# Prompt attention in a hybrid decoder step: each tile's scaling of its probabilities moved one place later in VectorE's order

## The reference

```
s = (q_lat . c + q_pe . k_pe) * MLA_SCALE
s = where(k_pos <= q_pos, s, -inf)
p = softmax(s)
out = p . c
```

## Time and profile before

| | us |
|---|---|
| timed runs | 1011.88, 1012.37, 1013.96 |
| median | 1012.37 |
| profiled execution, its time | 1013.96 |
| profiled execution, its span in the trace | 1012.2 |
| granted TensorE clock, mean over the span | 0.987 of 2.4 GHz |

### The profile page before, as it was taken

How to read it: one execution, slowest core, us unless ns; L and a number is a source line. 1 busy time by engine, 2 the same in 40 slices (tenths; PEclk the granted TensorE clock), 3 DMA queues, 4 the chain that set the end, 5 groups by cost and what they waited for, 6 DMA issues and landing times.

```text
span 1012.2 us, 20658 instructions
## 1 busy us (share of the span) xinstructions
PE 974.0 (96%) x8604; PEld 846.5 (84%) x8604; DVE 513.6 (51%) x980; ACT 444.4 (44%) x964; POOL 157.2 (16%) x257
## 2 busy tenths in 40 slices
PE   4999999999988999999999999999999999999997
PEld 3988899877756656666665999999999999999996
DVE  5655766666467387545546443533343344334333
ACT  5545638566644776544445324421332133113212
POOL 1020500155530301354550000000000000000000
PEclk9999969999999999999999999999999999999999
DMA  7312111030023602577772322332222222222202
GB/s 251 120 51 84 43 42 42 14 99 10 2 53 95 250 1 75 194 238 247 272 239 93 128 72 76 105 104 84 84 84 84 84 84 84 88 101 104 84 1 89
DMA packets 31655, 102.58 MB, mean 101 GB/s; under 512 B 14023, under 2 KB 14967, under 8 KB 25218
## 3 DMA queue, kind: packets, MB, share of 16 engines
q1 hardware_dynamic: 22346, 63.50, 19.1%
q0 software_dynamic: 9216, 37.75, 11.0%
HBM read 96.45 MB, written 4.22 MB: 99 GB/s over the span
## 4 chain that ended last, share of the span: by engine, by line
PE 90%; DVE 3%; ACT 3%; issue 1%; DMA 1%; SPq 0%; DVEq 0%; ACTq 0%
PE PS L598 17%; PE PS L600 17%; PE PS L599 17%; PE PS L1082 7%; PE PS L1093 3%; PE PS L1119 3%; PE PS L733 2%; PE PS L988 2%; PE PS L1102 1%; PE PS L806 1%; PE PS L837 1%; PE PS L889 1%; PE PS L1026 1%; PE PS L1007 1%; DMA RAW<-in_w_stream 1%
## 5 line engine op out<-in xcount | busy, mean ns | idle before, releaser
L598 PE MATMUL PS<-XH,WH 128*128 128x272 f32 (+1 forms) x896 | 261.8, 292 | 0.0
L600 PE MATMUL PS<-XH,WL 128*128 128x272 f32 (+1 forms) x896 | 261.2, 291 | 0.0
L599 PE MATMUL PS<-XL,WH 128*128 128x272 f32 (+1 forms) x896 | 260.2, 290 | 0.0
L1255 ACT ACTIVATE WH<-RAW 128x2048 fp32r<-128x2048 f32 x46 | 88.0, 1913 | 195.9 <-PE PS L600 191.7
L598 PEld LDWEIGHTS PS<-XH,WH 128*128 128x128 f32 x896 | 169.7, 189 | 4.8 <-issue 4.2
L599 PEld LDWEIGHTS PS<-XL,WH 128*128 128x128 f32 x896 | 170.0, 190 | 0.0
L600 PEld LDWEIGHTS PS<-XH,WL 128*128 128x128 f32 x896 | 169.7, 189 | 0.0
L598 PE MATMUL PS<-NH,WH 128*128 128x272 f32 x512 | 149.2, 291 | 0.8 <-DVE WL L1771 0.8
L600 PE MATMUL PS<-NH,WL 128*128 128x272 f32 x512 | 147.7, 289 | 0.0
L599 PE MATMUL PS<-NL,WH 128*128 128x272 f32 x512 | 146.7, 287 | 0.0
L1771 DVE TENSOR_TENSOR WL<-RAW,WH 128x2048 fp32r<-128x2048 f32 (+2 forms) x51 | 108.6, 2129 | 67.0 <-ACT WH L1255 64.8
(11 more groups left out here) (336 smaller groups left out, 1539.8 us busy)
## 6 DMA issues: line engine op xcount, KB each, us to landing
RAW<-in_w_stream SPq DMA_DIRECT2D x47, 1024.0 KB, 4.8
XN<-in_hin SPq DMA_DIRECT2D x4, 512.0 KB, 6.5
out_y_p<-YO SPq DMA_DIRECT2D x4, 512.0 KB, 2.7
CST<-in_big SPq DMA_DIRECT2D x1, 1132.5 KB, 13.4
SS<-in_sstate SPq DMA_DIRECT2D x1, 1024.0 KB, 5.0
out_ssm_s<-SS SPq DMA_DIRECT2D x4, 256.0 KB
CN<-in_cache,IDX POOLq DMA_INDIRECT x64
WQN<-in_wq SPq DMA_DIRECT2D x3, 256.0 KB, 5.8
```

Of the source, the lines that this page charges most:

```text
L598: pe.matmul(PS[:, b, 0:n], wh, xh[:, k, c:c + n], start=(k == 0), stop=False)
L599: pe.matmul(PS[:, b, 0:n], wh, xl[:, k, c:c + n], start=False, stop=False)
L600: last = pe.matmul(PS[:, b, 0:n], wl, xh[:, k, c:c + n], start=False, stop=(k == DT - 1))
L1255: act.activation(WH[w % 2][:, :, :], RAW[w % 2][:, :, :], ACT.Copy).then_inc(sem("w_high"), 1)
```

## The change

In VectorE's program the loop of prompt attention gets another lookahead. scale_p(1) ahead of the loop goes, and the loop's first step becomes scale_p(n + 1) instead of scale_p(n + 2). The sequence was scalings and maxima S1, S2, M4, S3, M5, S4, M6 and so on, ending in S31, M33, S32, S33. It becomes S1, M4, S2, M5, S3, M6 and so on, ending in S30, M33, S31, S32, S33. The programs of the other engines stay as they are.

```diff
--- before.py
+++ after.py
@@ -2207,10 +2207,9 @@
             new_start(1)
             dve.wait_ge(sem("part_high"), 2)
             low(QRFL[:, :, :], QRF[:, :, :], QRFH[:, :, :]).then_inc(sem("part_low"), 1)
-            scale_p(1)
             for n in range(NS_):
-                if n + 2 < NS_:
-                    scale_p(n + 2)
+                if n + 1 < NS_:
+                    scale_p(n + 1)
                 if n + 4 < NS_:
                     maxima(n + 4)
             def cache_copy(n, u):
```

## The result

The changed kernel takes **1017.82 us** (median of 4 runs, 1017.28 to 1019.62) against 1012.12 us before (median of 4, 1011.58 to 1013.96): a ratio of 1.0056, with a 95% interval of 1.0045 to 1.0068, or +5.7 us (4.6 to 6.9). The forecast was 1018.2 us, +5.8. Of the 29 recorded executions of the changed kernel one, which is left out, took 1085.26 us at a mean granted clock of 0.844; the others have a mean clock of 0.982 to 0.991.

What follows compares the result with a forecast made beforehand. TensorE, 974.0 us of matmul in a 1012.2 us span, was taken as the bound. Start +1.11, repeats +1.29, +1.38, +1.39, end +1.01, less 0.4, gave +5.8 on 1012.37: 1018.2 us, range 1016.0 to 1020.4.

Steps and rivals of the forecast that it cites:

- The start: Start of the prompt attention loop: scaling 2, maximum 5 and scaling 3 now follow maximum 4, delaying transposes 3: +1.11 us.
- (c): Transposes 19 to 20, last piece of the eight-tile walk: unchanged, 1.67 us.
- The repeat: Eight tiles of the loop, walked from transposes 12: 11.30 us against 9.92, +1.38.
- part (a): Transposes 12 to 15: start 4.39 us apart where TensorE's own work is 3.40, idle 0.99.
- part (b): Transposes 15 to 19: start 5.24 us apart where TensorE's own work is 4.85, idle 0.39.
- The end: Loop's end: transposes 31 wait for scaling 31 behind maximum 33, +1.01 us; 0.4 comes back at transposes 32.
- The handover of 0.05: Passing a tile between engines in the loop: assumed 0.05 us each; bounds of 0 and 0.10 gave +4.8 to +7.0.
- rival 4: Scores ready earlier than modelled, 0.2 us less at each of four handovers, a repeat costs about 0.6: 1015 us; chance 0.04.
- the occupancy of VectorE: VectorE, busy 9.33 of 9.92 us with unchanged work, paces the loop, so no change: 1012.4 us; chance 0.07.
- ScalarE's waits for maxima: Earlier maxima in the loop could remove all 4.4 us of these waits if exponentials paced it: 1008.0 us; chance 0.03.
- rival 3: TensorE's clock falls to 1.2 GHz in the loop, one repeat at half clock: 1028 us; chance 0.04.
- the ring: In the loop, transposes n, scores n+4, maximum n+4, scaling n+2, transposes n+2 wait in turn, spanning two tiles: +1.38 a repeat.

Runs made afterwards that it cites:

- the first experiment: Changed kernel with the scores of tiles 5 to 31 issued one tile earlier, scores 4 ahead of the loop: ratio 1.0026 to the kernel before, +2.6 us.
- the control: Kernel before, VectorE's order untouched, with the scores of tiles 4 to 31 issued one tile earlier on TensorE: ratio 1.0008 to the kernel before, +0.8 us.

## Why the prediction was right

Each term against what the two traces show, from the start of one tile's transposes to that of another's:

| stretch | before | after | difference | forecast |
|---|---|---|---|---|
| transposes 0 to 4 | 4.41 | 5.66 | +1.25 | +1.11 |
| 4 to 12 | 10.01 | 11.37 | +1.36 | +1.29 |
| 12 to 20 | 9.92 | 11.36 | +1.44 | +1.38 |
| 20 to 28 | 9.91 | 11.36 | +1.45 | +1.39 |
| 28 to the cache | 7.38 | 8.02 | +0.64 | +0.61 |
| sum | 41.63 | 47.77 | +6.14 | +5.8 |

The mechanism is the one that was forecast, and each term holds to within 0.14 us. That the sum of +5.8 lies within 0.1 of the timed +5.7 is closer than the terms are, whose sum in the traces is +6.14; the interval of the timed difference, 4.6 to 6.9, holds both.

- **The place before the loop costs nothing**: right. Scaling 1 stands where it stood, and transposes 1 start 1.12 us behind transposes 0, as against 1.11.
- **The start**: right in kind, 0.14 short. Maximum 4 waited 0.49 us for scores 4. It then took 0.90 us to the next instruction (357.45 to 358.35), where I had put 0.81; and transposes 3 to 4 take 1.72 us instead of 1.67, as in (c) below.
- **The repeat**: part (a) measured 377.53 - 373.16 = 4.37 us (forecast 4.39), part (b) 382.80 - 377.53 = 5.27 (5.24), part (c) 384.52 - 382.80 = 1.72 (1.67). The small surplus is mostly in (c), which I had taken over from a packed sequence: behind transposes 19, which now start after a wait, scores 23 follow in 0.17 us (382.80 to 382.97), where they followed in 0.12.
- **The end**: transposes 31 started 400.60 - 395.88 = 4.72 us behind transposes 28 (4.71). Of the wait at transposes 32, 0.4 was to come back. From transposes 31 to the cache it now takes 403.90 - 400.60 = 3.30 us, before it took 399.64 less about 395.96 = 3.68, so 0.38 came back and the term held: +0.64 against +0.61.
- **The handover of 0.05**: held. In the repeat from transposes 12 the four are 0.04, 0.06, 0.03 and 0.05 us (from a printed start plus duration to the start that waited for it). Its bounds, which gave +4.8 to +7.0, were wider than needed, and rival 4, with 0.2 us less at each, falls.
- **Nothing behind the loop takes part**: the cache stage keeps its step of 9.42 us, as the last section shows.
- **The rivals**: the occupancy of VectorE told nothing of what the order was worth, and where it could have (less work, order of before) there was nothing to gain. The Trainium skill's rule (Perfetto Trace Analysis, Identifying the Most-Contended Engine) takes occupancy on VectorE as a fair measure of how close that engine is to its limit, and this loop agrees only in that VectorE was nearly full; the 5.7 us came without any change to its load. ScalarE's waits for maxima did fall, by 3.7 us, and the kernel got slower: they were not on the path. The granted clock in the loop stayed at 1.00, so rival 3 did not come about. But its ground was thin: I had compared the idle time with a stretch in which TensorE was half idle, and the run with scaling n+3 shows the clock falling in a loop where TensorE was busy 4.43 of 6.00 us.
- **What TensorE would show**: I wrote 1.0 us of idle before transposes 15; the trace prints 0.73. The rest is not printed as idle: 0.16 is the overlap of scores 18 with what follows in a packed sequence (0.39 printed, 0.23 from start to start), and 0.08 is lost ahead of transposes 14. The starts, which the sum used, are right.

The expectation that missed is that of the first experiment. It took nearly all of the ring for opened; the two tiles at the end, worth 0.85 us, were not, and a ring over three tiles still cost about 0.17 a repeat. Two other medians lie outside what was expected, with intervals that overlap it: the control (+0.8 us for 0 to 0.5) and the order for 16 steps (+3.9 for 2.8 to 3.5).

## What to carry to other kernels

Where engines hand tiles around in a fixed order, write for each wait how many tiles lie between its two ends, and close the ring: its length over the tiles that it spans is a bound on the pace, beside each engine's own work. Look at an engine's place in the order rather than at its busy share; here one place was worth 1.4 us in each 10, with not an instruction more. Moving a step has two sides, one ring for later and one for earlier, and the lookahead that is best lies between them, here 2, of the three that were run.

## What the runs showed of the hardware

**The clock can fall in a loop of short waits.** In the run with scaling n+3, no wait of TensorE's matmuls for a scaling from 356 to 402 us is longer than 1.2 us (the last row of its waits above; its weight loads waited up to 1.8), and still its clock fell for a while, to half speed (1.2 GHz) for some of the time, with no longer pause ahead of it. Stretches of that run:

```profile
376.00:382.00 6.00, 4.43 (x30) 2.20 (x26) 3.71 (x12) 2.93 (x13) 0.00 (x0) 1.00 0.00 0
382.00:388.00 6.00, 4.43 (x24) 3.06 (x25) 3.90 (x12) 2.82 (x10) 0.00 (x0) 0.72 0.01 1
388.00:394.00 6.00, 5.10 (x41) 2.99 (x39) 3.72 (x13) 3.31 (x12) 0.00 (x0) 1.00 0.01 3
```

In the six microseconds from 382 the mean granted clock is 0.72, with 4.43 of 6.00 us busy ahead of it as well as in it. The repeat that holds this stretch took 16.02 us, the one ahead of it, at full clock, 15.96: here, where TensorE waited anyway, the slower clock cost little. The clock fell again from about 404 and from about 414 us, the last time behind a pause of 2.13 us. In the changed kernel, with TensorE busy 36.33 of the 40.00 us from 358, it never did in the loop.

**Two profiles can be apart before the changed stretch begins.** Up to the loop the programs are the same, yet transposes 0 start at 358.01 us in the profile of before and at 356.13 in that of after. The stretches from 120 to 150 us, of before and then of after:

```profile
120.00:135.00 15.00, 13.02 (x61) 12.66 (x59) 14.37 (x27) 9.77 (x22) 2.27 (x2) 0.70 0.18 60
135.00:150.00 15.00, 15.00 (x72) 13.74 (x71) 5.71 (x15) 2.59 (x6) 0.00 (x0) 0.62 0.03 12
```

```profile
120.00:135.00 15.00, 13.03 (x61) 12.46 (x60) 14.33 (x27) 10.07 (x22) 2.27 (x2) 0.73 0.16 49
135.00:150.00 15.00, 15.00 (x76) 13.38 (x75) 6.35 (x17) 3.45 (x10) 0.00 (x0) 0.70 0.06 23
```

TensorE's clock is at 1.2 GHz for part of them. The clock missing from full speed is 15 x (0.30 + 0.38) = 10.2 us before and 15 x (0.27 + 0.30) = 8.6 after, 1.6 us of the 1.88. This is not shown to be the whole account. Two more runs have the same program up to there: that with scaling n+3 misses 8.6 us of clock in these stretches, like the changed kernel, and starts transposes 0 at 356.58; that with the order for 16 steps misses 10.2, like the kernel before, and starts them at 357.53. About 0.5 us either way stays open. The rest of the difference between the spans lies behind the loop: the cache stage steps by 9.42 us in both, but in the profile of before two of its steps took 9.68 and 9.70. What makes such a step 0.27 us longer, the traces do not tell. So 6.14 - 1.88 - 0.54 = 3.72 us is left, which is about the 3.6 between the profiled spans. A difference of two single profiles is not the price of a change; that of the changed stretch is.
